# Hybrid mixer block: one 512-column modulation chain per feature pair, low parts of h on VectorE, first transfers issued by ScalarE

## What is computed

```python
mod = (c @ w_ada[l] + b_ada[l])[:, None, :]
sh1, sc1, gt1, sh2, sc2, gt2 = jnp.split(mod, 6, axis=-1)
h = rms_norm(x, g_mix[l]) * (1.0 + sc1) + sh1
(a_q, a_k, a_v, conv_in, c_q, c_k, c_v, c_r, c_low,
 d_q, d_k, d_v, gate_logits) = jnp.split(h @ w_in[l], split_points, axis=-1)
...
x = x + gt1 * (merged @ w_out[l])
h = rms_norm(x, g_mlp[l]) * (1.0 + sc2) + sh2
x = x + gt2 * (jnp.square(jax.nn.relu(h @ w_up[l])) @ w_down[l])
```

## Time and profile before

| | us |
|---|---|
| median of 3 runs | 2315.87 |
| lowest, highest | 2311.99, 2331.14 |
| the profiled execution's own time | 2316.98 |
| its span, first to last instruction | 2315.3 |
| TensorE matmul busy | 2115.3 (91%) |
| VectorE, ScalarE, GpSimd busy | 972.6, 621.0, 589.0 |

### The profile page before, as it was taken

The page is one execution under the profiler, slowest core; times in us unless marked ns, Lnnn a source line. Parts: engine busy times, 40 slices in busy tenths (PEclk is TensorE's granted clock), DMA queues, the critical chain, the costliest instruction groups (busy, mean ns, idle before and its releaser), DMA issues. The chain is left out here.

```text
span 2315.3 us, 23981 instructions
## 1 busy us (share of the span) xinstructions
PE 2115.3 (91%) x9583; PEld 1675.9 (72%) x9583; DVE 972.6 (42%) x1166; ACT 621.0 (27%) x853; POOL 589.0 (25%) x269
## 2 busy tenths in 40 slices
PE   4999999996888785896999999689999999999999
PEld 3787888783766653435888888568888888888887
DVE  6637554017745934563211111345323333433434
ACT  4311211234642224553111111133212112112111
POOL 2312222216001500102222222120434334333332
PEclk8999999999988786998999999899999999999999
DMA  6354453324033012006222221240111111111112
GB/s 221 103 156 138 151 172 91 91 91 173 27 105 138 10 42 85 1 1 177 66 57 57 57 57 57 93 180 19 46 46 46 55 46 46 55 46 46 55 46 91
DMA packets 187865, 187.43 MB, mean 81 GB/s; under 512 B 7370, under 2 KB 154954, under 8 KB 187770
## 3 DMA queue, kind: packets, MB, share of 16 engines
q1 hardware_dynamic: 187600, 186.03, 25.3%
q10 hardware_dynamic: 170, 0.07, 0.0%
HBM read 148.17 MB, written 37.91 MB: 80 GB/s over the span
## 5 line engine op out<-in xcount | busy, mean ns | idle before, releaser
L572 PE MATMUL dn_ps<-h_hi,dn_hi 128*128 128x512 f32 (+1 forms) x608 | 240.9, 396 | 10.6 <-POOL h_lo L317 10.6
L574 PE MATMUL dn_ps<-h_hi,dn_lo 128*128 128x512 f32 (+1 forms) x608 | 237.8, 391 | 0.0
L573 PE MATMUL dn_ps<-h_lo,dn_hi 128*128 128x512 f32 (+1 forms) x608 | 237.6, 391 | 0.0
L1229 DVE TENSOR_TENSOR tl_x<-tl_x,tl_bank 128x512 f32<-128x512 f32 x256 | 173.1, 686 | 133.2 <-PE tl_bank L574 133.2
L1065 POOL TENSOR_TENSOR tl_w_lo<-tl_raw,tl_w_hi 128x1024 fp32r<-128x1024 f32 x64 | 153.4, 2398 | 230.3 <-ACT tl_w_hi L986 230.3
L572 PE MATMUL tl_bank<-tl_h_hi,tl_w_hi 128*128 128x512 f32 x512 | 199.5, 390 | 0.0
L573 PE MATMUL tl_bank<-tl_h_lo,tl_w_hi 128*128 128x512 f32 x512 | 199.2, 389 | 0.0
L574 PE MATMUL tl_bank<-tl_h_hi,tl_w_lo 128*128 128x512 f32 x512 | 199.2, 389 | 0.0
L572 PE MATMUL tl_bank<-tl_w_hi,tl_u_hi 128*128 128x512 f32 x512 | 199.2, 389 | 0.0
L573 PE MATMUL tl_bank<-tl_w_lo,tl_u_hi 128*128 128x512 f32 x512 | 199.2, 389 | 0.0
L574 PE MATMUL tl_bank<-tl_w_hi,tl_u_lo 128*128 128x512 f32 x512 | 199.2, 389 | 0.0
(11 more groups left out here) (308 smaller groups left out, 3957.2 us busy)
## 6 DMA issues: line engine op xcount, KB each, us to landing
ada<-w_ada_dram SPq DMA_DIRECT2D x24, 1024.0 KB, 7.3
dn_raw<-w_in_dram SPq DMA_DIRECT2D x38, 512.0 KB, 4.4
proj<-dn_out SPq DMA_DIRECT2D x72, 256.0 KB, 2.3
tl_raw<-w_up_dram SPq DMA_DIRECT2D x32, 512.0 KB, 3.8
tl_raw<-w_down_dram SPq DMA_DIRECT2D x32, 512.0 KB, 3.7
mg_raw<-w_in_dram SPq DMA_DIRECT2D x28, 512.0 KB, 4.5
wa_qk<-proj SPq DMA_DIRECT2D x6, 1024.0 KB, 15.5
mg_y_raw<-mix SPq DMA_DIRECT2D x10, 512.0 KB, 4.0
```

Of the source, the lines that this page charges most:

```text
L572: nc.tensor.matmul(out, w_hi[:, t, :], x_hi[:, t, :], start=begin, stop=False)
L573: nc.tensor.matmul(out, w_hi[:, t, :], x_lo[:, t, :], start=False, stop=False)
L574: mm = nc.tensor.matmul(out, w_lo[:, t, :], x_hi[:, t, :], start=False, stop=end)
L1229: nc.vector.tensor_tensor(x1[:, tt, cols], x1[:, tt, cols], bank[:, 4 + n % 4, :], ALU.add).then_inc(summed, 1)
```

## The change

A chunk of the opening now holds the shift and scale columns of a pair together: 512 columns in two transfers of 1 MB, four chunks instead of eight, one chain of eight steps each. The ring holds two such chunks (32 KB a partition instead of 24), and for the late chunks, still 256 columns, it is a ring of two as well. x_rows becomes a ring of three. Both chunks of the first two pairs are issued by ScalarE's queue, behind the small vectors and ahead of its table load; SyncE issues x tiles with the first three w_in tiles between them. `h_lo` is made by VectorE, between parts of the next pair's chain (three steps, low, two steps, low, three steps). The splits of the first three w_in tiles move between x tiles (after tiles 3, 5, 7). The small vectors are transposed behind turn(1), chain 0 runs two steps at a time after tiles 2 to 5, and chain 1 runs in pair 0. Square writes to a buffer of its own.

```diff
-ADA_RING = 3
-X_RING = 4
+ADA_RING = 2
+X_RING = 3
...
-    CHUNKS = [first + f for f in range(0, KT, ADA_COLS) for first in (M_SH1, M_SC1)]
-    CHUNKS += [m for m in range(M_GT1, N_MOD, ADA_COLS)]
-    OPEN_CHUNKS = 2 * KT // ADA_COLS
+    CHUNKS = [(M_SH1 + f, M_SC1 + f) for f in range(0, KT, ADA_COLS)]
+    OPEN_CHUNKS = len(CHUNKS)
+    CHUNKS += [(m,) for m in range(M_GT1, N_MOD, ADA_COLS)]
...
-        ada_sum = ctx.enter_context(nc.sbuf_tensor("ada_sum", [P, 2, ADA_COLS * P], F32))
+        ada_sum = ctx.enter_context(nc.sbuf_tensor("ada_sum", [P, 2, 2 * ADA_COLS * P], F32))
...
-        ada = at("ada", 0, [P, ADA_RING, KT, ADA_COLS * P])
-        raw_x = at("dn_raw_x", 24 * KB, [P, 2, KT, P])
...
-        hf = at("hf", 48 * KB, [P, 2, S])
+        ada = at("ada", 0, [P, ADA_RING, KT, 2, ADA_COLS * P])
...
         x_rows = at("x_rows", 88 * KB, [P, X_RING, D])
+        x_square = at("x_square", 100 * KB, [P, D])
+        hf = at("hf", 96 * KB, [P, 2, S])
...
             def load_chunk(n):
                 if n >= ADA_RING:
                     sp.wait_ge(ada_step, KT * (n - ADA_RING + 1))
-                column = CHUNKS[n] * P
-                sp.dma_start(ada[:, n % ADA_RING], ada_view[:, :, column:column + ADA_COLS * P]).then_inc(ada_in[n % ADA_RING], 16)
-
-            for tt in range(4):
+                for i, m in enumerate(CHUNKS[n]):
+                    sp.dma_start(ada[:, n % ADA_RING, :, i], ada_view[:, :, m * P:(m + ADA_COLS) * P]).then_inc(ada_in[n % ADA_RING], 16)
+
+            for tt in range(3):
                 load_x(tt)
-            load_chunk(0)
-            load_chunk(1)
-            for tt in range(4, TT):
-                load_x(tt)
-            load_chunk(2)
             dense.load(sp, 0)
+            load_x(3)
+            load_x(4)
             dense.load(sp, 1)
-            load_chunk(3)
+            load_x(5)
+            load_x(6)
             dense.load(sp, 2)
-            for n in range(4, OPEN_CHUNKS):
+            load_x(7)
+            for n in range(ADA_RING, OPEN_CHUNKS):
                 load_chunk(n)
             dense.load(sp, 3)
...
-            for f in range(KT):
-                pool.wait_ge(full_ready, f + 1)
-                pool.wait_ge(h_hi_ready, f + 1)
-                nc.gpsimd.tensor_tensor(k.h_lo[:, f, :], hf[:, f % 2], k.h_hi[:, f, :].bitcast(F32), ALU.subtract).then_inc(h_lo_ready, 1)
...
             act.dma_start(convw_rows[:, :], conv_w[0]).then_inc(vec_in, 16)
+            for n in range(ADA_RING):
+                for i, m in enumerate(CHUNKS[n]):
+                    act.dma_start(ada[:, n, :, i], ada_view[:, :, m * P:(m + ADA_COLS) * P]).then_inc(ada_in[n], 16)
             nc.scalar.preload_act_table_set("natural_log_exp_and_others")
...
-                nc.scalar.activation(hf[:, 0], x_rows[:, tt % X_RING], ACT.Square, accum_out=ss[:, tt:tt + 1]).then_inc(x_squared, 1)
+                nc.scalar.activation(x_square[:, :], x_rows[:, tt % X_RING], ACT.Square, accum_out=ss[:, tt:tt + 1]).then_inc(x_squared, 1)
...
                 root(tt)
                 if tt >= 1:
                     take(tt - 1)
+                if tt in (3, 5, 7):
+                    dense.split(act, tt // 2 - 1)
             take(TT - 1)
-            for j in range(OPENING):
-                dense.split(act, j)
...
             def sum_chunk(n):
                 pe.wait_ge(ada_step, KT * (n + 1))
-                summed_before = n - n % 2 if n < OPEN_CHUNKS else n
-                if summed_before:
-                    pe.wait_ge(mod_ready, summed_before)
-                for m in range(ADA_COLS):
-                    last = nc.tensor.matmul(ps_m[:, CHUNKS[n] + m:CHUNKS[n] + m + 1], ada_sum[:, n % 2, m * P:(m + 1) * P], k.ones[:, 0:1],
-                                            start=True, stop=True)
+                if n >= 1:
+                    pe.wait_ge(mod_ready, n)
+                for i, first in enumerate(CHUNKS[n]):
+                    for m in range(ADA_COLS):
+                        at = (i * ADA_COLS + m) * P
+                        last = nc.tensor.matmul(ps_m[:, first + m:first + m + 1], ada_sum[:, n % 2, at:at + P], k.ones[:, 0:1], start=True, stop=True)
                 last.then_inc(ada_done, 1)
 
...
-            pe.wait_ge(vec_in, 16 * n_vec)
-            nc.tensor.transpose(ps_v[:, 0:P], vec_rows[:, :], k.ident[:, :]).then_inc(vec_turned, 1)
-            for c2 in range(2):
-                last = nc.tensor.transpose(ps_v[:, P + 32 * c2:P + 32 * c2 + 31], convw_rows[:, c2 * P:(c2 + 1) * P], k.ident[0:31, 0:31])
-            last.then_inc(vec_turned, 1)
             for tt in range(TT):
                 turn(tt)
+                if tt == 1:
+                    pe.wait_ge(vec_in, 16 * n_vec)
+                    nc.tensor.transpose(ps_v[:, 0:P], vec_rows[:, :], k.ident[:, :])
+                    for c2 in range(2):
+                        last = nc.tensor.transpose(ps_v[:, P + 32 * c2:P + 32 * c2 + 31], convw_rows[:, c2 * P:(c2 + 1) * P], k.ident[0:31, 0:31])
+                    last.then_inc(vec_turned, 1)
             sum_chunk(0)
-            sum_chunk(1)
             for f in range(KT):
                 opening(f)
-                if f % 2 == 0 and f // 2 + 1 < KT // ADA_COLS:
-                    sum_chunk(f + 2)
-                    sum_chunk(f + 3)
+                if f % 2 == 0 and f // 2 + 1 < OPEN_CHUNKS:
+                    sum_chunk(f // 2 + 1)
...
+            def chain(n, first=0, last=KT):
+
+                width = len(CHUNKS[n]) * ADA_COLS * P
+                if first == 0:
+                    dve.wait_ge(ada_in[n % ADA_RING], ada_bytes(n))
+                    if n >= 2:
+                        dve.wait_ge(ada_done, n - 1)
+                for kt in range(first, last):
                     ck = k.cols[:, V_C + kt:V_C + kt + 1]
+                    total = ada_sum[:, n % 2, 0:width]
+                    part = ada[:, n % ADA_RING, kt].rearrange("p i c -> p (i c)")[:, 0:width]
                     if kt == 0:
-                        ins = nc.vector.tensor_scalar(ada_sum[:, n % 2], ada[:, n % ADA_RING, kt], ck, None, ALU.mult)
+                        ins = nc.vector.tensor_scalar(total, part, ck, None, ALU.mult)
                     else:
                         dve.wait_ge(ada_step, n * KT + kt)
-                        ins = nc.vector.scalar_tensor_tensor(out=ada_sum[:, n % 2], in0=ada[:, n % ADA_RING, kt], scalar=ck, in1=ada_sum[:, n % 2],
-                                                             op0=ALU.mult, op1=ALU.add)
+                        ins = nc.vector.scalar_tensor_tensor(out=total, in0=part, scalar=ck, in1=total, op0=ALU.mult, op1=ALU.add)
...
             def modulation(n):
-                dve.wait_ge(ada_done, n + 2 - n % 2 if n < OPEN_CHUNKS else n + 1)
-                m = CHUNKS[n]
-                nc.vector.tensor_tensor(k.mod[:, m:m + ADA_COLS], ps_m[:, m:m + ADA_COLS], k.cols[:, V_BADA + m:V_BADA + m + ADA_COLS],
-                                        ALU.add).then_inc(mod_ready, 1)
+                dve.wait_ge(ada_done, n + 1)
+                for m in CHUNKS[n]:
+                    last = nc.vector.tensor_tensor(k.mod[:, m:m + ADA_COLS], ps_m[:, m:m + ADA_COLS], k.cols[:, V_BADA + m:V_BADA + m + ADA_COLS],
+                                                   ALU.add)
+                last.then_inc(mod_ready, 1)
...
+            def low(f):
+                dve.wait_ge(full_ready, f + 1)
+                dve.wait_ge(h_hi_ready, f + 1)
+                nc.vector.tensor_tensor(k.h_lo[:, f, :], hf[:, f % 2], k.h_hi[:, f, :].bitcast(F32), ALU.subtract).then_inc(h_lo_ready, 1)
...
-            scale_rows(0)
-            dve.wait_ge(vec_turned, 2)
-            nc.vector.tensor_copy(k.cols[:, :], ps_v[:, 0:P]).then_inc(vec_taken, 1)
-            nc.vector.tensor_copy(k.taps[:, :, :], ps_v[:, P:P + 64].rearrange("p (c j) -> p c j", c=2)[:, :, 0:31]).then_inc(vec_taken, 1)
-            for tt in range(1, TT):
+            for tt in range(TT):
                 scale_rows(tt)
-                take(tt - 1)
-                if tt == 3:
+                if tt >= 1:
+                    take(tt - 1)
+                if tt == 2:
+                    dve.wait_ge(vec_turned, 1)
+                    nc.vector.tensor_copy(k.cols[:, :], ps_v[:, 0:P]).then_inc(vec_taken, 1)
+                    nc.vector.tensor_copy(k.taps[:, :, :], ps_v[:, P:P + 64].rearrange("p (c j) -> p c j", c=2)[:, :, 0:31]).then_inc(vec_taken, 1)
                     dve.wait_ge(vec_taken, 1)
-                    chain(0)
-                if tt == 5:
-                    chain(1)
+                    chain(0, 0, 2)
+                if 3 <= tt < 6:
+                    chain(0, 2 * tt - 4, 2 * tt - 2)
             take(TT - 1)
-            for n in range(0, OPEN_CHUNKS, 2):
-                if n >= 2:
-                    chain(n)
-                    chain(n + 1)
+            for n in range(OPEN_CHUNKS):
                 modulation(n)
```

(62 more changed lines are left out.)

## The result

| | before | after |
|---|---|---|
| median of 20 runs each, us | 2317.24 | 2333.64 |
| lowest, highest | 2309.83, 2337.79 | 2326.38, 2351.20 |
| span of the profiled execution | 2315.3 | 2327.6 |

The ratio estimated from these runs is 1.0054, with a 95% interval of 1.0028 to 1.0080: slower, by about half a per cent (the two medians are 0.7% apart). In both kernels some runs stand some 20 us apart from the others, 6 of 20 before (2330.97 to 2337.79) and 5 of 20 after (2346.83 to 2351.20), so that medians of few runs move by several us with their number. The forecast was 2313.4, faster by 2.5 us; the range 2300 to 2325 doesn't hold the measured time. The sign is that of rival (c).

A forecast was written before the change was run, and what follows sets the result against it. Modulation bounds the opening; afterwards TensorE is always busy, so nothing hides. Opening -11.6 and dense part +9.1 give -2.5 against the profiled 2316.98, so 2314.5; with the median 1.1 lower, 2313.4, range 2300 to 2325.

The forecast's parts named there:

- rival (c): Dense part: ring of two costs 1.3 to 3.6 us per odd late load, more than opening gives; 2329.5 at 3.6; chance 0.07.
- What bounds the kernel: Opening bound by modulation, not TensorE; TensorE then always busy, so opening gains and later gaps reach the end in full.
- Part 1: Opening pairs: wide chains and VectorE low parts cut the period from 13.0 to 9.9 us, first pair 10.9.
- T: End of the first scale in the opening: 38.8 us before, forecast 42.3.
- Part 2: Way to the first scale: ScalarE held by four loads, Square at 13.6 us, scale ending at 42.3, 3.5 later.
- the hold of 2.4 us: x tiles: one GpSimd dn_lo holding VectorE, not hidden under the ring's waits, adds 2.4 us before the first scale ends.
- Part 3: Dense part: ring of two makes odd late loads hold stores, copy and TensorE; seven gaps of 1.3 us, 9.1 in all.
- (a): Dense part: stores not held, or copy still in time, so only the opening's gain counts; 2304.3 us; chance 0.27.
- (b): Opening: ScalarE not held by its four loads, Square at 8.9 us, opening -16.3; 2308.7 us in all; chance 0.13.
- (d): Opening pairs: lower clock stays or 512-column steps cost twice 256; opening gives only 4 to 6; about 2320; chance 0.08.

The follow-up runs named there:

- experiment 1: The changed kernel with late chunks in a ring of four half slots, so late load i waits for chain(i-4): 2304.84 us, ratio 0.9948 to the kernel before.
- experiment 2: The kernel before with one edit, late chunks waiting for chain(i-2) instead of chain(i-3), ring of three kept: 2341.89 us, ratio 1.0135 to the unedited kernel.
- experiment 8: experiment 7 with the ring of x tiles four deep, Square's output in the place of a w_in tile not loaded yet: 2298.93 us, ratio 0.9914.
- experiment 6: experiment 1 with the first three splits of w_in back behind the last x tile: 2310.37 us, ratio 0.9943 to the kernel before.
- experiment 7: experiment 1 with ScalarE issuing only pair 0's loads and SyncE issuing pair 1's behind x tile 7: 2298.81 us, ratio 0.9903 to the kernel before.
- experiment 3: The changed kernel with SyncE issuing the two stores of tile j-2 ahead of the late load: 2309.5 us, ratio 0.9962 to the kernel before.
- experiment 9: The changed kernel with dn_out doubled, so a copy waits for the store two tiles back: 2304.46 us, ratio 0.9933 to the kernel before.
- experiment 10: The changed kernel with the two stores put between SyncE's wait for chain(i-2) and the late 1 MB load: 2304.55 us, ratio 0.9951 to the kernel before.

## Why the prediction was wrong

Step by step, as it put them:

- **What bounds the kernel.** Right. With the gaps gone (experiment 1), the opening's gain arrives at the end; with them (experiment 2), nearly all of the loss does too, 25.7 us.
- **Part 1.** Right in kind, 1.4 us too short over the four pairs. Step 0.77 and low 1.22 to 1.24 as said, pairs 10.06 instead of 9.9. The first took 12.0 instead of 10.9: the sums wait behind opening(0), which met the lower clock for longer than forecast (6.8 us instead of 5.8), and this wait was put at 0.9 and measured 3.0. From T to half(3, 0) it is 44.2 us instead of 42.8.
- **Part 2.** T was forecast at 42.3 and came at 42.26, but two errors cancel in that. The Square was 0.9 later (14.47), since the fourth load was let go only at 13.15, 7.1 us after the first was issued; the x tiles took 27.8 instead of 28.7. That the ring of three alone sets their pace, 8.7 us for three tiles, fell with experiment 8, and the hold of 2.4 us that was to add to it is 1.2 by experiment 6. (Root, scale and turn add up to 4.4 and not 4.35, which changes nothing.) The Trainium skill, "DMA: Bandwidth & Descriptors", section "Issuing engines are not separate DMA queues", calls issue time usually small beside the transfer. For two loads the trace agrees (1.04 us in experiment 7), for four it doesn't (7.07).
- **Part 3, the step that failed.** It said "TensorE starts 1.3 us late ... 7 x 1.3 = 9.1 us". Place, order and count were right; experiments 2, 3, 9 and 10 each break or make one link of its chain. Its size was wrong twice. The gap was 2.13: the load landed in 5.9 us and not 5.0, and the store 0.8 behind it, 6.2 after its own issue. The 5.0 came from a single load of the opening. The list of DMA issues of the kernel before, 100 to 520 us, had the loads that were meant, and they take longer; Part 3 had their figure only as its bound:

```profile
ada<-w_ada_dram SPq DMA_DIRECT2D x14, 1024.0 KB, 7.3
```

By that figure the gap would have been 3.6: the late loads after stand between the two, at a median of 5.9. Second, the lower clock behind a gap wasn't in Part 3 at all, though Part 1 priced it for the pairs (1.7 a time). It came after six of seven gaps, 10.1 us. So Part 3 is 14.9 + 10.1 = 25.0 instead of 9.1, and -10.2 + 25.0 = +14.8 for opening and dense part together, where the profiled executions differ by 12.3 and the medians by 16.4.
- **The rivals.** (a) and (b) fell: the stores are held, and so is ScalarE. (d) fell: the granted clock is 1.00 from 54 to 86.4 us, and a step takes 0.77. (c) is what happened, with its place and its side. It was to decide from 1.7 us each; the gap alone was over that, 14.9 against 10.2. That its upper price of 3.6 is also what a gap cost with its clock (25.0 / 7) is luck: it stood for a landing of 7.3 us and for full clock. I gave it 0.07 because "no other load is in flight then". That is no reason: the load itself is enough. Forecast and (c) were one mechanism with two prices, so the range had to reach (c)'s end at 2329.5 at least. If the clock falls behind a gap of 1.3 too, which no run shows, even the forecast's own gap would have cost 3.0 and tipped the sum.

## What to carry to other kernels

A wait that is put ahead of a large load in a program's order delays everything behind the load twice, by the wait and by the load's own transfer; where small stores that free a buffer stand behind it, issue them first (in experiments 3 and 10 one swap takes 25.4 us off the dense part). Price a gap of a TensorE that is never idle with what the clock does behind it, here 1.7 us on top of 2.1. And when a buffer is regrouped for one stage, look at how deep it is in the others: the same bytes as four half slots (experiment 1), with pair 1's loads issued behind the last x tile (experiment 7), turn a loss of 0.5% into a gain of 0.7% by the rows and 1% by the medians.

## What the runs showed of the hardware

- A gap of 1.98 to 2.27 us in a TensorE that was otherwise busy was followed by the 1.2 GHz level (granted clock 0.51 to 0.56 over 3.5 us) in 13 cases of 14, six in the kernel after and seven in experiment 2. The one exception is the first gap of the kernel after, 2.20 us long. Why it differs stays open; no run was made for it.
- Two 1 MB loads hold their issuer 1.04 us, four hold it 7.07: the first, issued at 6.08, lands 7.0 us later, and the fourth is let go by 13.15.
- A 256 KB store issued 0.4 us behind a 1 MB load on the same queue lands in 6.2 us, 4.6 us behind it in 3.4 (the kernel before), ahead of it in 2.1.
- What a GpSimd subtraction takes from VectorE's chain doesn't depend on the width of the step that it holds: two subtractions (5.2 us) cost a chain of 256-column steps 4.0 us (7.65 against 3.61) and one of 512 columns 4.0 (9.44 against 5.4). One step is held by each, for 2.5 us at 256 columns and 2.7 to 2.8 at 512.
